# Two attention stages and a hybrid stage: values one couple later in one group, and the middle of the hybrid reordered

## Reference, cut to what matters

```python
def neighbourhood_attention(x, w_qkv, w_o, rpb):      # stage 0, 16 heads of 64
    ...
        sc = einsum('bhqd,bhrkd->bhqrk', q_i, k_rows) + bias
        p = softmax(where(mask, sc, -inf))
        return einsum('bhqrk,bhrkd->bhqd', p, v_rows)
    return o @ w_o

def dilated_attention(x, w_qkv, w_o):                 # stage 2, three groups
    for window, dil in ((128, 1), (512, 4), (2048, 16)):
        o, lse = banded_attention(q * 64**-0.5, k, v, window // (2 * dil), slopes * dil)
    alpha = softmax(stack(lses)); o = sum(alpha * outs)
    return o @ w_o

def hybrid_mixing(h, w_in, ...):                      # stages 5 and 8
    proj = h @ w_in
    y_a = gla_mixer(...)      # gated linear attention, 64-token chunks
    y_b = fox_mixer(...)      # attention with forget gates
    y_c = ssd_mixer(...)      # state space: decays within a chunk, one state copied over
    y_d = short_conv_mixer(...)
    return concatenate([y_a, y_b, y_c, y_d]) @ w_out
```

## Time and profile before

| | us |
|---|---|
| median of 3 runs | 1813.0 (1812.98 to 1813.49) |
| the profiled execution, whole | 1810.33 |
| its span on the profile | 1808.2 |
| TensorE busy | 1794.3 |
| VectorE busy | 1193.9 |
| ScalarE busy | 975.2 |
| GpSimd busy | 85.6 |
| mean granted TensorE clock | 0.998 |

### The profile page before, as it was taken

One profiled execution on the slowest core, in us unless ns is written; L12 is line 12 of the kernel. 1 busy time (PEld: TensorE's weight loads), 2 busy tenths in 40 slices (PEclk: granted clock), 3 DMA queues, 4 the chain that ended last, 5 costly groups with the idle time before them and its releaser, 6 DMA issues.

```text
span 1808.2 us, 26159 instructions
## 1 busy us (share of the span) xinstructions
PE 1794.3 (99%) x10576; PEld 1564.0 (86%) x10576; DVE 1193.9 (66%) x1774; ACT 975.2 (54%) x1492; POOL 85.6 (5%) x161
## 2 busy tenths in 40 slices
PE   8999999999999999999999999999999999999999
PEld 7878888889998888888889898888888888888887
DVE  5767774646666587557755767876487648678773
ACT  6656554544444565456545555655465546456551
POOL 0000000302220000000001010000000001000000
PEclk9999999999999999999999999999999999999999
DMA  9425565554333455545553333555365535335552
GB/s 348 161 107 186 187 224 184 198 186 140 120 137 132 159 188 198 211 155 192 188 217 143 140 117 139 210 188 216 132 218 194 216 129 186 117 140 188 188 217 83
DMA packets 45080, 315.68 MB, mean 175 GB/s; under 512 B 5008, under 2 KB 5264, under 8 KB 7968
## 3 DMA queue, kind: packets, MB, share of 16 engines
q1 hardware_dynamic: 44640, 313.45, 47.7%
q10 hardware_dynamic: 288, 0.52, 0.1%
q0 software_dynamic: 32, 0.03, 0.0%
HBM read 312.94 MB, written 1.05 MB: 174 GB/s over the span
## 4 chain that ended last, share of the span: by engine, by line
PE 95%; DVE 2%; ACT 2%; DMA 1%; issue 0%; POOL 0%; ACTq 0%; DVEq 0%; SPq 0%
PE P L392 92%; PE P L653 1%; PE P L399 1%; DVE wl L1649 1%; ACT xx L1186 0%; DMA raw<-w_all 0%; DVE hcv L2045 0%; ACT wh L1158 0%; DVE xx L1676 0%; DVE hxn L2147 0%; DMA C<-cst 0%; PE P L976 0%; PE P L560 0%; PE P L1054 0%; ACT L1518 0%
## 5 line engine op out<-in xcount | busy, mean ns | idle before, releaser
L1649 DVE TENSOR_TENSOR wl<-raw,wh 128x2048 fp32r<-128x2048 f32 x291 | 664.3, 2286 | 234.6 <-ACT wh L1158 217.6
L1158 ACT ACTIVATE wh<-raw 128x2048 fp32r<-128x2048 f32 x291 | 553.1, 1904 | 245.3 <-PE P L392 212.4
L392 PE MATMUL P<-xx,wh 128*128 128x512 f32 (+1 forms) x3488 | 662.4, 344 | 0.0
L392 PEld LDWEIGHTS P<-xx,wh 128*128 128x128 f32 x3488 | 552.2, 190 | 80.3 <-issue 6.8
L392 PE MATMUL P<-xx,wl 128*128 128x256 f32 x2704 | 354.0, 283 | 0.0
L392 PEld LDWEIGHTS P<-xx,wl 128*128 128x128 f32 x2704 | 341.9, 192 | 5.8
L392 PE MATMUL P<-wh,xx 128*128 128x512 f32 x672 | 215.3, 395 | 2.1 <-ACT wh L1164 1.0
L1287 ACT ACTIVATE ft<-P 128x256 f32<-128x256 f32 x240 | 90.0, 382 | 227.5 <-PE P L392 227.4
L392 PE MATMUL P<-wh,fhh 128*128 128x512 f32 x528 | 206.2, 390 | 0.0
L392 PE MATMUL P<-wh,fhl 128*128 128x512 f32 x528 | 205.5, 389 | 0.0
L392 PE MATMUL P<-wl,fhh 128*128 128x512 f32 x528 | 205.5, 389 | 0.0
(11 more groups left out here) (300 smaller groups left out, 1300.6 us busy)
## 6 DMA issues: line engine op xcount, KB each, us to landing
raw<-w_all SPq DMA_DIRECT2D x289, 1024.0 KB, 4.8
nB<-rpb SPq DMA_DIRECT2D x4, 768.0 KB, 9.2
raw<-w_all SPq DMA_DIRECT2D x4, 512.0 KB, 5.1
fgb<-post SPq DMA_DIRECT2D x2, 512.0 KB, 5.6
out<-xs SPq DMA_DIRECT2D x4, 256.0 KB, 2.5
C<-cst SPq DMA_DIRECT2D x1, 769.0 KB, 8.2
xs<-x_in ACTq DMA_DIRECT2D x2, 256.0 KB, 3.9
xs<-x_in SPq DMA_DIRECT2D x1, 512.0 KB, 7.0
```

The costliest lines, as they stand in the source:

```text
L392: return t_.on.matmul(o, l, r, start=start, stop=stop, skip_group_check=True)
L1158: a.on.activation(wh[k][:, 0:w], raw[r][:, 0:w], ACT.Copy).then_inc(*hi.up((m,)))
L1649: v.on.tensor_tensor(wl[k][:, 0:w], raw[r][:, 0:w], wh[k][:, 0:w].bitcast(F32), ALU.subtract).then_inc(*lo.up(m))
```

## The change

In both attention stages the values of a couple (in `dil` of a half couple) are computed one couple (half couple) later, on PE directly behind the scores, in the same group of small matmuls. ACT and DVE take the outputs later to match. At the start the first weight split goes ahead of `turn(0, 0, 1)` on ACT and DVE. In `dil` the copies of group 1 go in the order of banks 3, 5, 6, 7. In the hybrid ACT loads the Silu table ahead of the split of tile m+8, takes the second exponential of LS behind the gate activations, and copies the state ahead of Exp, Ln and `hvz`; DVE does the low part of tile m+5 ahead of the third `feat`, and the low part of tile m+9 behind the fox copies.

```diff
 PE, na
                         if f >= 1:
                             scores_na(f - 1)
+                        if f >= 3:
+                            values_na(f - 3)
 
                     feat(0, 4 + f, f % 2, 0, 8, between)
                     held[f % 2] = [(va, "q", 0, f)]
-                    if f >= 2:
-                        values_na(f - 2)
 
                 def after(i, t):
                     if i == 0:
                         probs_na(6)
                         scores_na(7)
-                    if i == 2:
-                        values_na(6)
+                        values_na(5)
                     if i == 5:
                         probs_na(7)
+                        values_na(6)
 PE, dil
                                 scores_dil(2 * f - 2)
-                            if f and z == 2:
-                                values_dil(2 * f - 2)
+                                if f >= 2:
+                                    values_dil(2 * f - 4)
...
-                        if f >= 2 and z == 0:
-                            values_dil(2 * f - 3)
                         if f and z == 1:
                             probs_dil(2 * f - 2)
                             scores_dil(2 * f - 1)
+                            if f >= 2:
+                                values_dil(2 * f - 3)
...
                     if i == 0:
                         probs_dil(13)
                         scores_dil(14)
-                    if i == 1:
-                        values_dil(13)
+                        values_dil(12)
                     if i == 3:
                         probs_dil(14)
                         scores_dil(15)
-                    if i == 4:
-                        values_dil(14)
+                        values_dil(13)
                     if i == 7:
                         probs_dil(15)
+                        values_dil(14)
 ACT, na and dil
                 turn(0, 0, 0)
+                first_high(0)
                 turn(0, 0, 1)
-                first_high(0)
...
-                    if f >= 2:
-                        out_na(f - 2)
+                    if f >= 3:
+                        out_na(f - 3)
...
-                    for i in range(4):
+                    for i in ((2, 3, 0, 1) if z == 1 else range(4)):
                         a.on.activation(AD["dV"][:, z, i // 2, halfs(i % 2)], P[banks[i]][:, :], ACT.Identity, bias=0.0,
...
-                        if f >= 2 and z == 1:
-                            out_dil(f - 2)
...
+                        if f >= 2 and z == 2:
+                            out_dil(f - 2)
 ACT, hybrid
+                ahead(m + 6)
+                a.on.preload_act_table_set(SILU)
                 ahead(m + 7)
-                a.on.preload_act_table_set(SILU)
...
-                for t in range(2):
-                    a.wait_ge(*vh.of("lsum", s, t))
-                    a.on.activation(LS[:, halfs(t)], LS[:, halfs(t)], ACT.Exp).then_inc(*ah.up(("ls", s, t)))
+                a.wait_ge(*vh.of("lsum", s, 0))
+                a.on.activation(LS[:, halfs(0)], LS[:, halfs(0)], ACT.Exp).then_inc(*ah.up(("ls", s, 0)))
                 a.wait_ge(*th.of("gu", s))
...
+                a.wait_ge(*vh.of("lsum", s, 1))
+                a.on.activation(LS[:, halfs(1)], LS[:, halfs(1)], ACT.Exp).then_inc(*ah.up(("ls", s, 1)))
                 a.wait_ge(*ah.of("g1", s))
                 a.on.activation(g2[:, :], g1[:, :], ACT.Abs).then_inc(*ah.up(("g2a", s)))
+                a.wait_ge(*th.of("st", s))
+                a.on.activation(ST[:, :], P[4][:, 0:256], ACT.Copy).then_inc(*ah.up(("st", s)))
...
-                a.wait_ge(*th.of("st", s))
-                a.on.activation(ST[:, :], P[4][:, 0:256], ACT.Copy).then_inc(*ah.up(("st", s)))
                 probs(0)
 DVE (na and dil as on ACT: first_low ahead of turn(0, 0, 1); out_na(f - 3); out_dil at z == 2, behind the shares)
...
                 def attend(i):
                     if i == 0:
                         scores_na(7)
+                        out_na(5)
                     if i == 2:
                         shares_na(7)
+                    if i == 5:
                         out_na(6)
 DVE, hybrid
+                ahead(m + 4)
                 feat(xb[:, 4:6, 3:3 + S], 3, m + 3, ("xb", s, 2))
-                ahead(m + 4)
                 conv(2)
...
-                ahead(m + 8)
                 for t in range(2):
                     v.wait_ge(*th.of("ls", s, t))
...
+                ahead(m + 8)
                 v.wait_ge(*ah.of("g2l", s))
```

More of the change, by code:

```diff
@@ L1405, in attend @@
                         exps_na(7)
-                    if i == 2:
-                        out_na(6)
+                        out_na(5)
                     if i == 5:
                         probs_na(7)
+                        out_na(6)
                     if i == 7:
@@ L1449, in attend @@
                         exps_dil(14)
-                    if i == 1:
-                        out_dil(6)
                     if i == 3:
@@ L1454, in attend @@
                         exps_dil(15)
+                        out_dil(6)
                     if i == 7:
@@ L1935, in na @@
                 turn(0, 0, 0)
+                first_low(0)
                 turn(0, 0, 1)
-                first_low(0)
                 turn(0, 1, 0)
```

## The result

The changed kernel takes 1799.2 us (median of 4 runs, 1799.06 to 1799.52), the kernel before 1813.0 beside it; ratio 0.9924, 95% interval 0.9907 to 0.9941. That is 13.8 us faster. The profiled executions differ by less: 1799.52 against 1810.33, 10.8 us, and so do their spans, 1797.4 against 1808.2.

The account below looks back on a forecast made before the run. TensorE, busy 99% of the span, was taken as the bound. Terms -1.0 - 0.8 - 3.4 + 1.2 - 3.7 - 3.1 = -10.8 us took the median from 1813.0 to 1802.2; range 1798.0 to 1808.5.

Parts of the forecast that it names:

- Rival 5: The 2.7 us between profile and runs is the clock falling in stage 8 too, and goes: 1799.5; chance 0.10.
- Start, -1.0: At the start, four of ACT's eight x splits go behind the first weight split, so PE starts 1.0 us earlier.
- 0 if a load is late: Lower bound of the gain at the start: nothing if a load arrives late; the other bound is -1.1 us.
- Copies of group 1, -0.8: In `dil`, bank 3 copied first is free when PE wants it, so a stop of 0.76 us goes.
- Groups, 20 x 0.17: In `na` and `dil`, 20 groups of values behind scores save 0.17 us of switching each, -3.4 in all.
- little less: Each merged group was put at 0.17, under the 0.19 us outside, as a first pair may start dearer.
- Rival 2: Tile switches save nothing, values behind scores pay as much: 1805.6 us; chance 0.10.
- bound of 0.34: Most that a merged group of values could save, in us, if scores to values cost no switch.
- Later values: Delayed attention values: no stall in steady couples (slack 0.5 us `na`, 0.4 `dil`); ends cost +0.5 in `na`, +0.7 in `dil`.
- Rivals 3 and 4: Steady couples' slack is missing: 0.3 us in each of 17 groups, 1807.3, chance 0.11; or large, 1816.6 or above, chance 0.04.
- Hybrid, -3.7: In the hybrid stages, the Silu stop (0.5 us) and both state copy stops (2.7) go, plus 0.5 for lost overlap.
- Clock, -3.1: In stage 5, the half clock behind the state wait goes with the stop, -3.1 us; bounds 0 and -3.1.

Follow-up runs that it names:

- second profile of before: The kernel before, run again with no edit: 1812.0 us (11 runs), its profiled execution with a span of 1810.5 us.

## Why the prediction was right

The forecast was 1802.2, the time is 1799.2: faster, as said, inside the range, and 3.0 below the likeliest value. Of the rivals, the fifth came true on top of the forecast. That the sum for the profiled execution came out to 0.03 us is partly luck: the start fell short by 0.5 and the ends cost 0.2 more, while the groups brought 0.4 more and the small terms the rest.

**What bounds it.** Right. Every microsecond gained is TensorE's stream or a stop in it.

**Start, -1.0: half of it.** The order of work was read rightly; the bound "0 if a load is late" is what bit. In the five profiles with the new order and one load ACT's first split waits for the load, and the first matmul starts at 8.68 to 9.17, on average 8.88, against 9.35 to 9.71, on average 9.44, in the six with the old one. The prediction didn't look for when that load landed. In the profile before it was 7.83 us, only 0.1 ahead of when the new order would want it; in the five it is 7.88 to 8.38, and the profiled execution of the changed kernel has the latest. What the prediction didn't know: three of the six profiles with the old order have the low clock at the start, 0.8 to 1.1 us more; none of the five has. That the shorter stop is why is likely and was not shown by itself: with the start edit alone 3 of 11 runs lie in the upper cluster, against 31 of the 58 of the kernel before.

**Copies of group 1, -0.8.** Right, -0.87.

**Groups, 20 x 0.17.** Right in mechanism; size 0.19 in `dil` and 0.17 to 0.19 in `na`. Nearly the whole 0.19 outside is saved. The "little less" that I took off for a dearer first pair isn't there: the values' first matmuls cost the same behind scores as behind a half. Rival 2, that switches save nothing, is out, and so is the bound of 0.34: the inner 0.16 stays.

**Later values.** The slack in steady couples was counted as 0.5 in `na`: shares now end at 91.58 + 0.62 = 92.20 and PE wants them at 92.74, 0.54. Rivals 3 and 4 needed it gone. The end of `dil` was right (0.71). The end of `na` was 0.67 in place of 0.5, and for another reason in part. The timelines of TensorE and DVE there, after:

```profile
99.23 0.39 PE L392 MATMUL P<-wh,nol 128*128 128x512 f32 x1
99.71 0.50 PE L392 MATMUL P<-wh,noh 128*128 128x512 f32 x1
...
100.52 1.35 PE L653 MATMUL P<-C,npA 128*128 128x128 f32 x8
101.80 1.13 PE L392 MATMUL P<-nq 64*128 64x256 f32 x8
...
98.96 0.69 DVE L1956 TENSOR_TENSOR nq<-P,nrb 128x512 f32<-128x512 f32 x1 [2.10 <-PE P L392]
...
100.48 0.62 DVE L1893 TENSOR_SCALAR npA<-npA,nsmA 128x256 f32<-128x256 f32 x2
```

The shares cost 0.32 (the eight transposes take 1.28 to the next start in place of 0.96). The other 0.35 is PE waiting for `nq` to free its bank at 99.65 (0.25, and 0.10 for the matmul behind it, which then starts 0.33 later in place of 0.23): before, a group of values stood between the end of `feat` and these matmuls and covered it. The prediction reckoned with that bank in `dil` and missed it in `na`.

**Hybrid, -3.7.** Right: Silu -0.72, the stops at the state gone. One reason was idle: the earlier sums of decays aren't needed, the copy alone does it. Another isn't settled: the attention edits alone took the stop behind Silu away too.

**Clock, -3.1.** Right, and too small in scope. The difference between the first profile and the median (2.7) was taken as fixed. The second profile of before is 2.3 longer than the first, and all of it is clock and start: the fall in stage 8 (1.6) and the start (0.8: 1.1 of low clock less 0.3 of an earlier first matmul). The other 0.4 no profile shows. Rival 5 named the first and sized it at the whole 2.7. It had a chance of 0.10 where more was due: the stop in stage 8 was of the same kind (1.1 us against 1.6). The prediction's own argument, that the fall follows the gap at once, doesn't hold: the stop ended at 1024.77, and the clock stays full for 1.5 us of matmuls behind it (windows of before, columns as in the earlier trace rows):

```profile
1024.80:1026.30 1.50, 1.50 (x9) 1.14 (x9) 0.00 (x0) 0.00 (x0) 0.00 (x0) 1.00 0.00 0
```

What bears the term is the experiment that filled the stop.

The Trainium skill, TensorE: Matmul & The Clock Gate, section HAM oscillation, has the clock fall only behind gaps longer than any here that stands between matmuls (only the wait for the first load, 4.1 us, ahead of the whole stream, is longer than 1.7). The runs disagree with it: filling a stop of 1.6 us, with nothing else changed, took the fall away.

## What to carry to other kernels

When TensorE is busy 99% of the span, look at the stops that stand just ahead of a stretch at low clock: one copy of 0.4 us, moved ahead of 2.5 us of other work on ACT, was worth 8.5 us here, about half of it clock. If the copy can't be moved, a dozen empty matmuls in the stop bring the clock's part. A gap between one profile and the median of runs is a term of the sum too, so ask what can vary before you hold it fixed.

Groups of small matmuls that use part of the array are cheapest side by side; and when work moves out of a place, list what it covered there.

## What was unexpected in the hardware

The granted clock falls to 0.50, 0.9 to 2.2 us after the end of a TensorE stop of only 1.1 to 1.6 us, though not always: in the four profiles that have the stops at the state's copy, it fell each time in stage 5 (once behind 1.1 us, for 6.8 us) and three times of four in stage 8 (behind 1.1 us, for some 3.3 us). It never fell behind the stops of 0.3 to 0.9 us of these profiles. Why it falls in one execution and not in another is open. At the start the same code runs at low clock until 13 to 14 us or not at all, which is 0.8 to 1.1 us of spread that no edit makes.

Going from 64-row to 64-column groups costs no more than the arrival from full-array matmuls: values take 1.01 to 1.02 us in both places, and it is the full-array halves on either side that pay 0.09 to 0.10 each.

A 512 KB load split in two of 256 KB was complete 0.9 to 1.4 us later than as one, beside the same other transfers.
